# First products take the rounded half before the low half, and three things move out of the norms' chain

## The reference

```python
for i in range(2):                                   # first stack
    proj = rmsnorm(h, norm_g[i]) @ w_in[i]
    ...                                              # gated recurrence and block-sparse attention on proj
    h = h + concat([y_hg, y_nsa]) @ w_out[i]
    gate = sigmoid(rmsnorm(h, ple_norm_g[i]) @ w_pg[i])
    h = h + gate * (p[i] @ w_pp[i])
...
# second stack; every part ends in a layer_norm of alpha * h + part(h)
# per layer: swiglu_ffn, differential attention (layer 0) or pool_mixer (layer 1),
#            memory_cross_attention, swiglu_ffn
def rmsnorm(x, g):
    var = mean(x * x, -1);  return x * rsqrt(var + 1e-6) * g
def layer_norm(x, g, b):
    mu = mean(x, -1);  var = mean((x - mu) ** 2, -1)
    return (x - mu) * rsqrt(var + 1e-5) * g + b
```

## Time and profile before

| | us |
|---|---|
| median of 3 runs | 3324.89 |
| lowest and highest | 3307.03, 3327.67 |
| the profiled execution's own time | 3316.13 |
| span of its trace | 3314.3 |
| PE busy | 3080.1 (93%) |
| POOL busy | 1362.9 (41%) |
| DVE busy | 1159.3 (35%) |
| ACT busy | 1101.8 (33%) |

### The profile page before, as it was taken

How to read it: one execution, slowest core, us unless ns; L and a number is a source line. 1 busy time by engine, 2 the same in 40 slices (tenths; PEclk the granted TensorE clock), 3 DMA queues, 4 the chain that set the end, 5 groups by cost and what they waited for, 6 DMA issues and landing times.

```text
span 3314.3 us, 58641 instructions
## 1 busy us (share of the span) xinstructions
PE 3080.1 (93%) x24246; PEld 2815.0 (85%) x24246; DVE 1159.3 (35%) x1921; ACT 1101.8 (33%) x1823; POOL 1362.9 (41%) x656
## 2 busy tenths in 40 slices
PE   7998998999888999989889989998999978989998
PEld 7986587987578999979469789998999957789997
DVE  1535742444743211052751532103211084441202
ACT  4233633223633222231633332223222133342222
POOL 5534044443132545444026245444445444254543
PEclk9999998999999999999889999999999998999999
DMA  5211023212012223222013122232233231123231
GB/s 188 70 64 52 1 67 106 77 45 70 14 51 66 95 95 102 95 75 89 15 64 115 63 76 95 95 102 76 90 100 102 95 108 59 56 76 101 94 103 57
DMA packets 72202, 262.23 MB, mean 79 GB/s; under 512 B 8032, under 2 KB 8672, under 8 KB 70912
## 3 DMA queue, kind: packets, MB, share of 16 engines
q1 hardware_dynamic: 69728, 249.77, 22.8%
q10 hardware_dynamic: 2336, 10.49, 0.9%
HBM read 258.13 MB, written 2.10 MB: 79 GB/s over the span
## 4 chain that ended last, share of the span: by engine, by line
PE 83%; DVE 10%; ACT 3%; issue 2%; POOL 1%; DMA 0%; POOLq 0%; ACTq 0%; DVEq 0%
PE bank L502 23%; PE bank L504 23%; PE bank L506 23%; PE bank L627 1%; PE bank L800 1%; PE bank L832 1%; PE bank L1040 1%; PE bank L816 1%; POOL wl L376 1%; DVE s L1623 1%; PE bank L678 1%; PE bank L590 1%; PE bank L1031 1%; PE bank L870 1%; DVE small L2029 1%
## 5 line engine op out<-in xcount | busy, mean ns | idle before, releaser
L376 POOL TENSOR_TENSOR wl<-raw,wh 128x1024 fp32r<-128x1024 f32 x464 | 1153.9, 2501 | 1854.7 <-ACT wh L1107 1854.7
L502 PE MATMUL bank<-xh,wh 128*128 128x256 f32 x5120 | 1033.9, 284 | 78.2 <-POOL xl L390 56.8
L504 PE MATMUL bank<-xl,wh 128*128 128x256 f32 x5120 | 1013.7, 280 | 0.0
L506 PE MATMUL bank<-xh,wl 128*128 128x256 f32 x5120 | 1012.1, 280 | 0.0
L502 PEld LDWEIGHTS bank<-xh,wh 128*128 128x128 f32 x5120 | 790.0, 192 | 109.2 <-issue 108.7
L1107 ACT CAST wh<-raw 128x1024 fp32r<-128x1024 f32 x464 | 471.9, 1049 | 1094.4 <-PE bank L506 1047.7
L504 PEld LDWEIGHTS bank<-xl,wh 128*128 128x128 f32 x5120 | 788.1, 191 | 0.0
L506 PEld LDWEIGHTS bank<-xh,wl 128*128 128x128 f32 x5120 | 785.8, 191 | 0.0
L1438 ACT ACTIVATE sg<-bank 128x512 f32<-128x512 f32 x88 | 52.7, 599 | 683.4 <-PE bank L506 683.4
L1965 DVE TENSOR_TENSOR tb<-sg,bank 128x512 f32<-128x512 f32 x88 | 60.6, 688 | 614.9 <-ACT sg L1438 614.9
L506 PE MATMUL bank<-hh,wl 128*128 (+1 forms) x1408 | 274.2, 276 | 0.0
(11 more groups left out here) (323 smaller groups left out, 3283.2 us busy)
## 6 DMA issues: line engine op xcount, KB each, us to landing
raw<-in_slabs SPq DMA_DIRECT2D x464, 512.0 KB, 3.3
h<-in_x_t SPq DMA_DIRECT2D x8, 256.0 KB, 5.3
w1v<-in_w ACTq DMA_DIRECT2D x2, 1024.0 KB, 4.9
side<-in_pp_w ACTq DMA_DIRECT2D x2, 1024.0 KB, 5.0
xm<-in_mem_t ACTq DMA_DIRECT2D x2, 1024.0 KB, 4.8
out<-h SPq DMA_DIRECT2D x8, 256.0 KB, 2.0
side<-in_w SPq DMA_DIRECT2D x1, 1024.0 KB, 12.6
vt<-in_p_t ACTq DMA_DIRECT2D x2, 512.0 KB, 5.9
```

The costliest lines, as they stand in the source:

```text
L376: nc.gpsimd.tensor_tensor(wl[:, n % RING, :], raw[:, n % RING, :], wh[:, n % RING, :], A.subtract).then_inc(w_low, 1)
L502: nc.tensor.matmul(dst[:, c], high_l, high_r[:, c], start=first and n == 0, stop=False)
L504: nc.tensor.matmul(dst[:, c], high_l, low_r[:, c], start=False, stop=False)
L506: out = nc.tensor.matmul(dst[:, c], low_l, high_r[:, c], start=False, stop=last and n == len(parts) - 1)
```

## The change

- **Order of the first products.** `pair` with waits, and `token_major`, now take the two passes that need only `xh` (high by high, high by low weight) as soon as `xh` of a chunk is there, and the pass with `xl` later: in `pair` after the high passes of the next chunk, in `token_major` after those of the slab's second chunk. The waits count `xh` and `xl` apart. `products` no longer waits for `xl` ahead of its loop. Number and size of the matmuls stay.
- **`xh` before `h`.** In an `ln`, ACT writes `xh` first and `h` second; POOL waits for both (`hn` is a new count).
- **One statistics product less.** After `w_out` and `ffn_out`, ACT writes the square of chunk 6 into a free PSUM bank, DVE adds it to the square of chunk 7 (`e2`), and PE makes one product of the sum instead of two. The product of `s1` stands ahead of that of `s2` and waits for its own count.
- **Table.** The load of the inverse root's table moves from the norm to the start of `w_out`, `ffn_out` and `pool`, behind the last sigmoid in `pg`, and to the program's start.
- **Conversions.** In the last step of `w_out` one of the two casts moves behind the squares; in `pg` the last step's casts move behind the sigmoids, one before and one behind the squares; in `ffn_out` one cast moves ahead of the squares and one out of the norm's wait.

The diff, without the counts and the like:

```diff
@@ -308,6 +309,10 @@
 
+        def last_even_square(kind):
+            return bank[0 if kind == "ffn_out" else 7][:]
...
@@ -387,6 +392,8 @@
                     pool.wait_ge(S["xh"], st["xh"] + c + 1)
+                    if st["kind"] == "ln":
+                        pool.wait_ge(S["hn"], st["hn"] + c + 1)
...
@@ -510,14 +517,38 @@
 
-            def pair(slab, kind, act_h, act_l, w, waits):
-                for k in range(KC):
-                    waits(k)
-                    for o in range(2):
-                        a, b = tile_of(slab + o, k)
-                        last = passes(bank[2 * kind + o][:, 0:w], a, b, act_h[:, k, :], act_l[:, k, :],
-                                      k == 0, k == KC - 1)
+            def part(dst, terms, first, last):
+                w = dst.shape[1]
+                cut = w // 2 if w == T else w
+                cols = [slice(a, a + cut) for a in range(0, w, cut)]
+                for i, (fixed, moving) in enumerate(terms):
+                    for n, c in enumerate(cols):
+                        out = nc.tensor.matmul(dst[:, c], fixed, moving[:, c], start=first and i + n == 0,
+                                               stop=last and i == len(terms) - 1 and n == len(cols) - 1)
+                return out
+            def pair(slab, kind, act_h, act_l, w, high_in=None, low_in=None):
+                banks = [bank[2 * kind + o][:, 0:w] for o in range(2)]
+                for k in range(KC if low_in is None else KC + 1):
+                    if low_in is None:
+                        if high_in is not None:
+                            high_in(k)
+                        for o in range(2):
+                            a, b = tile_of(slab + o, k)
+                            last = passes(banks[o], a, b, act_h[:, k, :], act_l[:, k, :], k == 0, k == KC - 1)
+                        continue
+                    if k < KC:
+                        high_in(k)
+                        for o in range(2):
+                            a, b = tile_of(slab + o, k)
+                            part(banks[o], ((a, act_h[:, k, :]), (b, act_h[:, k, :])), k == 0, False)
+                    if k:
+                        low_in(k - 1)
+                        for o in range(2):
+                            a, _ = tile_of(slab + o, k - 1)
+                            last = part(banks[o], ((a, act_l[:, k - 1, :]),), False, k == KC)
...
                     pe.wait_ge(took_v, ticket)
-                if split_base is not None:
-                    pe.wait_ge(S["xl"], split_base + 1)
+                def high_in(k):
+                    pe.wait_ge(S["xh"], split_base + k + 1)
+                def low_in(k):
+                    pe.wait_ge(S["xl"], split_base + k + 1)
 
                 def two(i):
                     for j in range(2):
@@ -535,10 +570,8 @@
                             pe.wait_ge(took_a, i * 2 + (ticket + j - 1))
                             pe.wait_ge(took_v, i * 2 + (ticket + j - 1))
 
-                        def waits(k):
-                            if split_base is not None and j == 0:
-                                pe.wait_ge(S["xl"], split_base + k + 1)
-                        pair(slab + 2 * j, j, act_h, act_l, w, waits).then_inc(prod, 1)
+                        two_steps = (high_in, low_in) if split_base is not None and j == 0 else ()
+                        pair(slab + 2 * j, j, act_h, act_l, w, *two_steps).then_inc(prod, 1)
...
-                        c = 2 * s + k
+                    n = (slab + s) % RING
+                    steps = [(2 * s, False), (2 * s, True), (2 * s + 1, False), (2 * s + 1, True)]
+                    if split_base is not None:
+                        steps = [(2 * s, False), (2 * s + 1, False), (2 * s, True), (2 * s + 1, True)]
+                    for c, low in steps:
                         if split_base is not None:
-                            pe.wait_ge(S["xl"], split_base + c + 1)
-                        n = (slab + s) % RING
+                            pe.wait_ge(S["xl" if low else "xh"], split_base + c + 1)
+                        k = c % 2
                         b_h, b_l = wh[:, n, k * 512:k * 512 + w], wl[:, n, k * 512:k * 512 + w]
                         for t in range(tiles):
                             ts = slice(t * P, (t + 1) * P)
-                            last = passes(bank[banks + t][:, 0:w], act_h[:, c, ts], act_l[:, c, ts], b_h, b_l,
-                                          c == 0, c == KC - 1)
+                            terms = ((act_l[:, c, ts], b_h),) if low else ((act_h[:, c, ts], b_h), (act_h[:, c, ts], b_l))
+                            last = part(bank[banks + t][:, 0:w], terms, c == 0 and not low, c == KC - 1 and low)
...
@@ -570,9 +606,10 @@
                 b_mean, b_sq, _ = stat_banks(st)
+                if st["kind"] == "ln":
+                    pe.wait_ge(S["s2" if st["pooled"] else "s1"], st["s2" if st["pooled"] else "s1"])
+                    nc.tensor.matmul(b_mean, mean_m, s1, start=True, stop=False)
                 pe.wait_ge(S["s2"], st["s2"])
-                if st["kind"] == "ln":
-                    nc.tensor.matmul(b_mean, mean_m, s1, start=True, stop=False)
                 nc.tensor.matmul(b_sq, mean_m, s2, start=True, stop=False)
                 if st["kind"] == "ln":
                     for c in (KC - 2, KC - 1):
@@ -582,6 +619,10 @@
                             pe.wait_ge(took_v, st["took"])
                         last = nc.tensor.matmul(b_mean, mean_m, h[:, c, :], start=False, stop=(c == KC - 1))
                     last.then_inc(S["stat"], 1)
+                if not st["own_sq"]:
+                    pe.wait_ge(S["e2"], st["e2"])
+                    nc.tensor.matmul(b_sq, mean_m, sq[:, 1, :], start=False, stop=True).then_inc(S["stat"], 1)
+                    return
...
@@ -1128,20 +1168,17 @@
                         act.wait_ge(S["s2"], st["s2"] + c - 1)
-                    nc.scalar.activation(sq[:, c % 2, :], h[:, c, :], F.Square
-                                         ).then_inc(took_a if c % 2 else S["sq"], 1)
+                    nc.scalar.activation(last_even_square(st["kind"]) if c == KC - 2 else sq[:, c % 2, :], h[:, c, :],
+                                         F.Square).then_inc(took_a if c % 2 else S["sq"], 1)
 
...
                 b_mean, b_var, b_y = stat_banks(st)
-                table(F.Abs_reciprocal_sqrt)
                 act.wait_ge(S["stat"], st["stat"] + 1)
...
                 if st["before"] == "ffn_out":
-                    for k in range(1, TAIL):
-                        high(st["slab"] - TAIL + k + RING)
+                    high(st["slab"] - 1 + RING)
...
@@ -1159,8 +1196,8 @@
                         else:
-                            nc.scalar.activation(h[:, c, :], v, F.Identity, bias=b)
                             nc.scalar.activation(xh[:, c, :], v, F.Identity, bias=b).then_inc(S["xh"], 1)
+                            nc.scalar.activation(h[:, c, :], v, F.Identity, bias=b).then_inc(S["hn"], 1)
...
@@ -1404,24 +1441,32 @@
             def w_out(st):
+                table(F.Abs_reciprocal_sqrt)
                 for j in range(4):
                     act.wait_ge(prod, st["prod"] + j + 1)
                     high(st["slab"] + 2 * j + RING)
-                    high(st["slab"] + 2 * j + RING + 1)
+                    if j < 3:
+                        high(st["slab"] + 2 * j + RING + 1)
                     pair_squares(st, j)
+                high(st["slab"] + 7 + RING)
 
...
                     act.wait_ge(prod, st["prod"] + j + 1)
-                    high(st["slab"] + 2 * j + RING)
-                    high(st["slab"] + 2 * j + RING + 1)
+                    if j < 3:
+                        high(st["slab"] + 2 * j + RING)
+                        high(st["slab"] + 2 * j + RING + 1)
                     if j:
...
                     nc.scalar.activation(sg[:, 1, :], bank[2 * (j % 2) + 1][:], F.Sigmoid).then_inc(took_a, 1)
+                    if j == 3:
+                        table(F.Abs_reciprocal_sqrt)
+                        high(st["slab"] + 2 * j + RING)
                     squares(st, 2 * j)
                     squares(st, 2 * j + 1)
+                high(st["slab"] + 7 + RING)
...
@@ -1453,8 +1499,10 @@
                     act.wait_ge(prod, st["prod"] + NF - TAIL + j + 1)
+                    if j == 3:
+                        high(st["slab"] + NF - TAIL + RING)
                     pair_squares(st, j)
-                high(st["slab"] + NF - TAIL + RING)
+                high(st["slab"] + NF - TAIL + RING + 1)
...
@@ -1925,10 +1974,18 @@
                 if j == 3:
+                    dve.wait_ge(S["sq"], st["sq"] + 4)
+                    dve.wait_ge(took_a, st["took"] + 4)
+                    V.tensor_tensor(sq[:, 1, :], last_even_square(st["kind"]), sq[:, 1, :], A.add).then_inc(S["e2"], 1)
                     return
                 if ln:
                     for o in range(2):
```

(10 more changed lines are left out.)

36 lines of the change are left out of this document (17 added, 19 removed).

## The result

The changed kernel takes 3275.85 us in the median of 4 runs (3267.46 to 3283.95), the kernel before, beside it on the same chip, 3326.28 (3307.03 to 3332.60): a ratio of 0.986, 95% interval 0.981 to 0.990. Predicted were 3277 us. The profiled execution took 3269.5 us, its span is 3267.7; before it was 3314.3, so 46.6 us have gone.

The account below looks back on a forecast made before the run. PE bounds the kernel, so time is gained only where it stands still. Savings of 25.7 + 9.4 + 4.9 + 4 = 44 us give 3272 from the profiled 3316.1, 3281 from the median; forecast 3277, range 3256 to 3303.

Parts of the forecast that it names:

- Part A: At first products behind norms and splits, PE starts on xh instead of waiting for xl: 25.7 us saved.
- The three pieces: Behind an ln before a loop: xh before h 0.6, POOL's subtraction 1.3, loop entry some 0.4 us; 2.4 each.
- the 1.7 of layer 1: At pg in layer 1, table load and one cast no longer precede the split's xh in ACT's queue: 1.7 us.
- about 55: Sign in the changed profile: PE's wait at first products shrinks from 91.5 us to about 55.
- The extra waits: Some 490 waits in 61 pairs: taken as 0, far bound 22 us; rival if exposed 3299, chance 0.18 shared.
- Part B: Shorter statistics in norms: 2.6 us behind w_out, 5.7 behind ffn_out, 1.1 at two rms norms; 9.4 us saved.
- Part C: End of pg, sigmoids ahead of casts: 3.2 us in layer 0, 1.7 in layer 1; 4.9 us saved.
- upper bound of 4.7: Layer 0's pg gain if casts, DVE's additions and the squares' half clock all improve: 4.7 us; casts alone 2.0.
- Part D: First pairs: shorter PE stops leave two to four of 13 at full clock; 4 us saved, -6 if unlucky.
- the low clock after a norm lasts longer: Sign that would prove the forecast wrong: after a norm, PE's low clock lasts longer than before; no size given.
- the head start given back: Rival at 13 first pairs: longer half clock loses 2 us each; gain 18 us, 3307; chance 0.18 shared with exposed waits.
- PE run in bursts: Rival at 13 first pairs: stops for low halves keep the clock at half; 60 us slower, 3385; chance 0.04.

Follow-up runs that it names:

- order_alone: The kernel before with only the new order of first products and its waits, h still written ahead of xh: 3298.67 us, ratio 0.993.
- waits: The changed kernel with each wait for xh and xl in the products loops made four times: 3278.92 us, ratio 0.986.
- stats_undone: The changed kernel with the old statistics and cast places behind w_out and ffn_out, the table load still out of the norm: 3292.15 us.
- table_back: The changed kernel with the table load back at the head of the norms behind w_out and ffn_out: 3276.04 us.
- pg_undone: The changed kernel with the old last step of pg, both casts ahead of the sigmoids and the table load behind the squares: 3275.07 us.
- after_more: The changed kernel, unchanged, run again in a later batch: 3277.05 us (6 runs), its profiled span 3309.8 us.
- fill: The changed kernel plus products of constants into a free bank during PE's stops: 3283.80 us (4 runs); repeated, 3274.97 us (6 runs).

## Why the prediction was right

- **Part A, 25.7 us.** Measured in the stops: 2.39 at each of five loops (12.0), 1.98 at `da_project`, 5.6 at the four rms norms, 4.5 at four splits, and 1.2 at the fifth (`order_alone`, 9.51 to 8.27): 25.3. The three pieces were sized rightly; what part A did not say is that the 0.65 for `xh` ahead of `h` exists only with the new order. The wait at first products that part A's sum implies, 91.5 less 25.7 and less the 1.7 of layer 1, is 64 us, and 64.6 came; the "about 55" among the signs did not follow from the sum.
- **The extra waits, 0.** In the changed kernel they leave one step in each of 58 pairs and otherwise ride on matmuls and their weight loads; `waits` has 32 more steps a pair and loses nothing in the pairs.
- **Part B, 9.4.** 8.8 by `stats_undone`. The terms that were off are `ffn_out`, 1.35 a place, not 1.5, because PE's product starts 0.06 us after DVE's addition and takes 1.13, not 1.0; the `rms` norms, 0.42, not 0.56; and the last norm, 1.36, not 1.2. That the load counts only once the statistics are shorter was right (`table_back`).
- **Part C, 4.9.** 4.5 to 4.9: 3.0 and 1.9 between the profiles of before and after, 2.6 and 1.9 by `pg_undone`. The squares stayed at half clock in the first profile; where they don't (1.99 us in `after_more`), layer 0 gains about as much as the upper bound of 4.7.
- **Part D, 4.** The 15 first pairs are 6.1 us shorter in sum. As forecast, four of them stay fast. The size came out, but partly by luck: at three of the six norms of kind `ln` the pair spent more time at half clock than before, in sum 23.5 us against 26.2, so the sign "the low clock after a norm lasts longer" was seen at half of them.
- These are 45 us of the 46.6. The rest is not one small term: outside these places single stretches differ by -2.9 to +4.6 us, by pace and clock, and nearly cancel. **The rivals:** no first pair of the profile after took over 13.8 us, so neither was the head start given back nor did PE run in bursts. The Trainium skill, "TensorE: Matmul & The Clock Gate", "HAM oscillation — how this bites in real kernels", tells of such bursts, with waits of some 3 to 5 us between them. Here PE does wait inside the pairs, 0.13 us in the changed kernel (11.77 us, 11.64 busy) and 0.47 in `fill` (12.20, 11.73 busy), and the clock stayed at 1.00; waits as long as the page's are not in these pairs.
- **Where luck helped.** One draw of the pace in a feed-forward stage is 13 us, as much as parts B and C together. A profiled run like that of `after_more`, with a span of 3309.8 us, would have shown 4.5 us.

## What to carry to other kernels

Let the consumer start on the half of a split operand that is made first; that alone took 20.9 us from the stops here. Reorder the producer together with that, since by itself the reordering was worth nothing (8.55 us of stop against 8.48). A hidden step (a table load, a cast) becomes the bound as soon as its cover is shortened, so cost it against the cover that will be left. Before 1% is read from a total, compare the same stage in both traces. The feed-forward stages here agree to 0.02 us between profiles at the same pace, whatever was changed elsewhere; a stage that was not changed and still takes 13 us more tells of the pace and not of the edit.

## What was not expected of the hardware

At a granted clock of 1.00 matmuls of 256 columns follow each other either every 113.3 ns (10.88 us for 96) or every 117.8 ns (11.31), and a feed-forward stage of some 3000 keeps its pace, 13.2 us apart. With the lowest runs 5.7 us apart and the medians in reverse, the spread that this makes is wider than what separates the changed and the filled kernel. What sets it stays open: DVE's and ACT's times beside it are the same (the windows above have even less DMA in the slow stage, 0.26 against 0.29), and no run here changed it on purpose.
